# Page loads spread over the second block, raw weight halves loaded one stage ahead, 64-row products paired, and the samples' steps begun with the attention

## The reference

```
xn = rms_norm(x, norm_in)
u  = einsum('btd,dc->btc', xn, w_in)           # 2048 -> 12016 columns
u_a, u_b, u_m = split(u, [A_COLS, A_COLS + B_COLS])
o_a = rwkv7_mixer(u_a, ...)                    # 16 heads of 64, state S updated token by token
o_b = nsa_mixer(q, gates, cmp_kv, sel_kv, win_kv, ...)   # compressed, selected and window attention
h = x + (sig(gate_a) * (o_a @ w_pa) + sig(gate_b) * (o_b @ w_pb)) @ w_o
y = rms_norm(h, norm_out)
```

## Time and profile before

| | us |
|---|---|
| three runs | 2744.36, 2750.11, 2754.10 (median 2750.11) |
| the profiled execution | 2745.68 |
| its span | 2743.9 |

### The profile page before, as it was taken

The page is one execution under the profiler, slowest core; times in us unless marked ns, Lnnn a source line. Parts: engine busy times, 40 slices in busy tenths (PEclk is TensorE's granted clock), DMA queues, the critical chain, the costliest instruction groups (busy, mean ns, idle before and its releaser), DMA issues. The chain is left out here.

```text
span 2743.9 us, 50970 instructions
## 1 busy us (share of the span) xinstructions
PE 2391.9 (87%) x21174; PEld 2171.8 (79%) x21174; DVE 1192.3 (43%) x2330; ACT 797.1 (29%) x1495; POOL 439.7 (16%) x236
## 2 busy tenths in 40 slices
PE   5999999999999999778998789999815664999996
PEld 4998989898888989678997778888703334999996
DVE  4244544545454544336776434444414334443223
ACT  4342333333332332112221154445301112232211
POOL 0000000000000000000110049999800000000000
PEclk8999999999999999989999889999957885999998
DMA  3221212122121222166665422222175714332332
GB/s 121 91 84 61 71 62 76 64 76 76 56 81 61 71 73 79 59 203 210 209 224 183 147 58 79 60 76 67 56 237 176 222 47 162 140 140 106 103 110 89
DMA packets 123373, 299.56 MB, mean 109 GB/s; under 512 B 23962, under 2 KB 37028, under 8 KB 117412
## 3 DMA queue, kind: packets, MB, share of 16 engines
q1 hardware_dynamic: 104820, 252.93, 28.0%
q0 software_dynamic: 7360, 29.74, 3.1%
q10 hardware_dynamic: 10992, 14.05, 1.4%
HBM read 259.45 MB, written 45.54 MB: 111 GB/s over the span
## 5 line engine op out<-in xcount | busy, mean ns | idle before, releaser
L164 PE MATMUL acc<-xh,w_hi 128*128 128x272 f32 x1824 | 415.2, 309 | 21.9 <-DVE xl L419 11.1
L146 DVE TENSOR_TENSOR w_lo<-w_raw,w_hi 128x1024 fp32r<-128x1024 f32 x166 | 203.1, 1224 | 504.0 <-ACT w_hi L137 485.0
L164 PE MATMUL acc<-xh,w_lo 128*128 128x272 f32 x1824 | 378.8, 289 | 0.0
L164 PE MATMUL acc<-xl,w_hi 128*128 128x272 f32 x1824 | 378.5, 289 | 0.0
L164 PEld LDWEIGHTS acc<-xh,w_hi 128*128 128x128 f32 x1824 | 286.0, 190 | 58.2 <-issue 32.7
L137 ACT ACTIVATE w_hi<-w_raw 128x1024 fp32r<-128x1024 f32 x188 | 198.5, 1056 | 415.5 <-DMA w_raw<-in_w_all 197.4
L164 PEld LDWEIGHTS acc<-xl,w_hi 128*128 128x128 f32 x1824 | 288.8, 190 | 0.0
L164 PEld LDWEIGHTS acc<-xh,w_lo 128*128 128x128 f32 x1824 | 287.2, 190 | 0.0
L164 PE MATMUL b_acc<-xh,w_hi 128*128 128x272 f32 x800 | 174.3, 300 | 48.1 <-DVE w_lo L146 28.6
L164 PEld LDWEIGHTS b_acc<-xh,w_hi 128*128 128x128 f32 x800 | 131.2, 197 | 51.1 <-DVE w_lo L146 30.0
L164 PE MATMUL b_acc<-xl,w_hi 128*128 128x272 f32 x800 | 170.6, 296 | 0.0
(11 more groups left out here) (397 smaller groups left out, 4374.7 us busy)
## 6 DMA issues: line engine op xcount, KB each, us to landing
w_raw<-in_w_all SPq DMA_DIRECT2D x188, 512.0 KB, 3.6
b_rows<-in_cmp_rows SPq DMA_DIRECT2D x128, 256.0 KB, 3.2
d_kv<-in_sel_kv SPq DMA_DIRECT2D x128, 256.0 KB, 2.8
m_w<-in_w_mo SPq DMA_DIRECT2D x32, 1024.0 KB, 5.8
m_gates<-tmp_uT SPq DMA_DIRECT2D x16, 544.0 KB, 3.8
out_s_win<-in_win_in POOLq DMA_DIRECT2D x8, 1016.0 KB, 5.8
tmp_uT<-ub POOLq DMA_DIRECT2D x24, 272.0 KB, 2.3
tmp_uT<-ub ACTq DMA_DIRECT2D x23, 272.0 KB, 2.1
```

The costliest lines, as they stand in the source:

```text
L146: eng.tensor_tensor(self.T.Wl[h % N_SPLIT][:, :, :], self.T.raw[h % N_RAW][:, :, :], self.T.Wh[h % N_SPLIT][:, :, :].bitcast(F32), ALU.sub ...
L164: ins = self.nc.tensor.matmul(acc[:, c, 0:HALF], w[:, k % KH, :], x[:, k, c * HALF:(c + 1) * HALF], start=(k == 0 and m == 0), stop=(k == ...
```

## The change

The changed kernel alters four things.

- The raw halves of the next block are loaded at the end of the block before (`h_load`, two more than `h_ahead`), and SP waits for them there (`landed`).
- In `rwkv`, the products that use 64 rows only are issued in turns on rows 0 to 63 and 64 to 127: `G` (L897) and `W2` (L932). The last pair's pieces shrink from 48 to 36, and 12 pieces are left for behind `var`.
- In `rest`, the pages of a sample are loaded four at a time, one group of four per half, and each behind the raw half's load. The constants come behind the first four. The pooling begins at half 4, not 3.
- In `attend_prompt`, keys and queries lie on both row halves, so that `S0` uses rows 0 to 63 and `S1` rows 64 to 127, one right behind the other. The first row is loaded by ACT, the samples' data by POOL, the values have a semaphore of their own; the samples' preparation on ACT and DVE comes ahead of the first row, and 12 pieces come ahead of the first score instead of 7.

```diff
-        self.h_ahead = min(self.h1 + 2, 2 * N_CHUNK)
+        self.h_ahead, self.h_load = (min(self.h1 + n, 2 * N_CHUNK) for n in (2, 2 + N_RAW))
         self.ready = 0 if first == 0 else 2
+        self.loaded = 0 if first == 0 else 2 + N_RAW
...
+    def landed(self, sp):
+        for j in range(N_RAW):
+            sp.wait_ge(self.w_in[j], 16 * len([h for h in range(self.h0 + self.loaded, self.h_load) if h % N_RAW == j]))
...
-        before = [m for m in range(self.ready, n + 1) if (m + self.h0) % N_RAW == h % N_RAW]
-        act.wait_ge(self.w_in[h % N_RAW], 16 * len(before))
+        before = [m for m in range(self.loaded, n + 1) if (m + self.h0) % N_RAW == h % N_RAW]
+        if before:
+            act.wait_ge(self.w_in[h % N_RAW], 16 * len(before))
...
+        at, span = 0, pair if i < 7 else pair - LAST_PIECES
         for name, b0, nb, eng, gap in PAIR_JOBS:
             at += gap
...
-            place[i, name] = at
+            place[i, name] = FIRST_PIECES + pair * i + at * span // pair
...
+            W.landed(sp)
...
-                background(place[i, "var"])
+                background(place[i, "var"] + (LAST_PIECES if i == 7 else 0))
...
-                def g_quarter(q):
-                    job(i, f"G{q}")
-                    hp = H[q // 2]
+                def g_half(q):
+                    job(i, f"G{2 * q}")
+                    job(i, f"G{2 * q + 1}")
                     for n in range(4):
-                        nn = 4 * (q % 2) + n
-                        ins = mm(bank[:, bank_of[i, f"G{q}"], n * P:(n + 1) * P],
-                                 BK[hp, nn, :, :].rearrange("p a c -> p (a c)"),
-                                 KR[hp, nn, :, :].rearrange("p a c -> p (a c)"), start=True, stop=True)
-                    done(ins)
-                g_quarter(0)
-                g_quarter(1)
+                        for h, hp in enumerate(H):
+                            ins = mm(bank[:, bank_of[i, f"G{2 * q + h}"], n * P:(n + 1) * P],
+                                     BK[hp, 4 * q + n, :, :].rearrange("p a c -> p (a c)"),
+                                     KR[hp, 4 * q + n, :, :].rearrange("p a c -> p (a c)"), start=True, stop=True)
+                            if n == 3:
+                                done(ins)
+                g_half(0)
...
-                for h, name in enumerate(("W2a", "W2b")):
-                    job(i, name)
-                    for n in range(NCH):
+                job(i, "W2a")
+                job(i, "W2b")
+                for n in range(NCH):
+                    for h, name in enumerate(("W2a", "W2b")):
                         ins = mm(bank[0:CH, bank_of[i, name], n * CH:(n + 1) * CH], mats["Tt"][H[h], n, :],
                                  mats["X2"][H[h], n, :], start=True, stop=True)
-                    done(ins)
+                        if n == NCH - 1:
+                            done(ins)
...
-UNIT_AT, UNIT_END, PROMPT_AFTER = 3, 47, 1
+UNIT_AT, UNIT_END, PROMPT_AFTER = 4, 47, 1
...
+            def pages(b, q):
+                if b >= 2 and q == 0:
                     sp.wait_ge(x_used, b - 1)
-                for p in range(N_PAGES):
+                for p in range(4 * q, 4 * q + 4):
                     page = sp.value_load(table[0:1, b * N_PAGES + p:b * N_PAGES + p + 1], min_val=0, max_val=N_POOL - 1)
                     sp.dma_start(X[b % 2][:, p, :, :], A["cmp_rows"][bass.ds(page, 1)].rearrange("a c s x -> (a c) s x"))\
                         .then_inc(rows_in[b % 2], 16)
             for h in range(W.h0, W.h1):
-                if h + 4 < W.h_ahead:
+                if h + 4 < W.h_load:
                     W.load(sp, h + 4)
-                if h - W.h0 < 2:
-                    pages(h - W.h0)
-                for b in range(2, DEC_B):
-                    if ended[b - 2] == h - W.h0:
-                        pages(b)
+                for b in range(DEC_B):
+                    q = h - W.h0 - (4 * b if b < 2 else ended[b - 2] + 1)
+                    if 0 <= q < 4:
+                        pages(b, q)
+                if h == W.h0:
+                    for dst, src in ((pos_s, "pos_s"), (pos_w, "pos_c"), (wbd, "wbd"), (w_kv, "w_kv")):
+                        sp.dma_start(dst[:], A[src]).then_inc(consts, 16)
+            W.landed(sp)
...
-PROMPT_PIECES, START_PIECES = PIECES * (N_CHUNK - KEY_CHUNKS), 7
+PROMPT_PIECES, START_PIECES = PIECES * (N_CHUNK - KEY_CHUNKS), 12
...
+        def load_row(eng, w):
+            g, r = ROWS[w]
+            j = w % 2
+            row = COL_Q + w * HD
+            for k in range(2):
+                eng.dma_start(q[j][k * HD:(k + 1) * HD, :], A["uT"][row:row + HD, 0:SEQ]).then_inc(row_in[j], 16)
+            eng.dma_start(bias[j][:, :], A["bias_p"][g, :, r, :]).then_inc(row_in[j], 16)
+            eng.dma_start(cbias[j][:, :, :], A["cbias_p"][g, :, N_TILE * r:N_TILE * (r + 1), :]).then_inc(row_in[j], 16)
...
+            load_keys(0)
+            load_values(0)
+            load_row(sp, 1)
...
+            load_samples(pool)
             between()
             samples_steps(pool, between)
...
+            load_row(act, 0)
+            c = COL_GATE - 48 * P
+            act.dma_start(gates[:, :, :], A["u_tok"][:, :, c:c + N_GATE]).then_inc(gates_in, 16)
+            background(4)
+            samples_act(act)
+            background(8)
+            act.wait_ge(gates_in, 16)
+            f(gates[:, :, :], gates[:, :, :], ACT.Sigmoid).then_inc(gates_ready, 1)
+            act.wait_ge(gates_ready, 1)
...
+            samples_dve(dve)
             row_maxes(0)
             maxes(0)
...
+                banks = [job(f"S{k}", u) for k in range(2)]
+                for k, rows in enumerate((slice(0, HD), slice(HD, P))):
+                    done(mm(banks[k][:, 0:keys(t)], q[w % 2][rows, t * P:(t + 1) * P], kT[w // REP % 2][rows, 0:keys(t)],
                             start=True, stop=True))
...
+                if t == 0 and w % REP == 0:
+                    pe.wait_ge(values_in[w // REP % 2], 16 * N_VALUES_IN * (w // REP // 2 + 1))
```

More of the change, by code:

```diff
@@ L216, in job_tables @@
     jobs = [(-1, *j) for j in FIRST_JOBS]
-    place, at = {}, FIRST_PIECES
+    place, pair = {}, sum(j[4] for j in PAIR_JOBS)
     for i, name, *_, where in jobs:
@@ L338, in background @@
             def background(upto):
-                while loads[0] < W.h_ahead and HALF_PIECES * (loads[0] - 4) <= upto:
+                while loads[0] < W.h_load and HALF_PIECES * (loads[0] - 4) <= upto:
                     W.load(sp, loads[0])
@@ L1026, in _ @@
             sp.dma_start(table[:, :], A["page_table"]).then_inc(table_in, 16)
-            for h in (W.h0 + 2, W.h0 + 3):
-                W.load(sp, h)
-            for dst, src in ((pos_w, "pos_c"), (wbd, "wbd"), (pos_s, "pos_s"), (w_kv, "w_kv")):
-                sp.dma_start(dst[:], A[src]).then_inc(consts, 16)
             sp.wait_ge(table_in, 16)
-            def pages(b):
-                if b >= 2:
+            def pages(b, q):
+                if b >= 2 and q == 0:
                     sp.wait_ge(x_used, b - 1)
-                for p in range(N_PAGES):
+                for p in range(4 * q, 4 * q + 4):
                     page = sp.value_load(table[0:1, b * N_PAGES + p:b * N_PAGES + p + 1], min_val=0, max_val=N_POOL - 1)
@@ L1276, in load @@
         eng.dma_start(tab[:, :, :], A["stab"]).then_inc(loaded, 16)
-        eng.dma_start(S[:, :, :], A["state"]).then_inc(loaded, 16)
+        eng.dma_start(S[:, :, :], A["state"]).then_inc(state_in, 16)
     def store(eng):
@@ L1288, in act_before @@
         f = nc.scalar.activation
-        act.wait_ge(loaded, 48)
+        act.wait_ge(loaded, 32)
         f(w[:, :, :], sw, ACT.Exp, scale=DECAY_SCALE).then_inc(act_done, 1)
@@ L1336, in dve_before @@
         vv.memset(eps[:, :], GN_EPS)
-        dve.wait_ge(loaded, 48)
+        dve.wait_ge(loaded, 32)
         link(tt(kraw[:, :, :], k, over_t(0), ALU.mult))
@@ L1434, in attend_prompt @@
         W = Projection(nc, A, T, acc, "a", KEY_CHUNKS, N_CHUNK)
-        q, bias = [sb(f"a_q{j}", [HD, SEQ]) for j in range(2)], [sb(f"a_bias{j}", [P, SEQ]) for j in range(2)]
+        q, bias = [sb(f"a_q{j}", [P, SEQ]) for j in range(2)], [sb(f"a_bias{j}", [P, SEQ]) for j in range(2)]
         cbias = [sb(f"a_cbias{j}", [P, N_TILE, N_CMP_PAD]) for j in range(2)]
-        kT = [sb(f"a_kT{j}", [HD, 2, SEQ]) for j in range(2)]
+        kT = [sb(f"a_kT{j}", [P, SEQ]) for j in range(2)]
         vv = [sb(f"a_v{j}", [P, 2, N_TILE, HD]) for j in range(2)]
@@ L1447, in attend_prompt @@
         out = [sb(f"a_out{j}", [P, N_TILE, REP, HD]) for j in range(2)]
-        row_in, group_in = [sem(f"a_row_in{j}") for j in range(2)], [sem(f"a_group_in{j}") for j in range(2)]
+        row_in, keys_in, values_in = ([sem(f"a_{n}{j}") for j in range(2)] for n in ("row_in", "keys_in", "values_in"))
         gates_in, gates_ready, zeroed = sem("a_gates_in"), sem("a_gates_ready"), sem("a_zeroed")
@@ L1491, in load_group @@
```

(26 more changed lines are left out.)

44 lines of the change are left out of this document (20 added, 24 removed).

## The result

The changed kernel takes 2652.05 us (median of four runs, 2649.62 to 2653.21) against 2751.64 for the kernel before (four runs): ratio 0.9636, 95% interval 0.9616 to 0.9657. The forecast was 2647, with 2620 to 2690 as its range. The profiled execution took 2649.62 us, with a span of 2647.8 against 2743.9.

What follows compares the result with a forecast made beforehand. It took TensorE (PE), busy 87%, as the bound. Terms of -55 (`rest`), -17 (`rwkv` pairing), -1 (last pair) and -28 (attention) sum to -101: 2745.68 to 2644.7 us, plus half of 4.4, forecast 2647, range 2620 to 2690.

Steps and rivals of the forecast that it cites:

- Pages in `rest`: In `rest`: pages in fours between raw halves end PE's waits behind SP's queue; -55 us, of 42.7 idle and 21.0 low clock.
- The fit that was doubted: In `rest`: DVE's 239.5 to 255.6 us of work fits PE's 258.6 over 43 halves, by only 1 to 7%.
- Rivals C and D: In `rest`: DVE or late pages pace it, 2670 us, chance 0.17; or short waits keep the clock low, 2780 us, 0.04.
- Pairing in `rwkv`: In `rwkv`: `G` and `W2` in turns on both row halves overlap, taking 13.0 and 6.0 us less; counted as -17.
- the deduction for shorter cover: In `rwkv`: shorter products cover less of DVE's work behind them, so -17 us was taken of 19.
- Rival B: In `rwkv` and attention: products on two row halves with the same 128 columns do not overlap; 2677 us, chance 0.12.
- Last pair and gap: End of `rwkv`: fewer pieces cost +4.6 us, twelve held back cut the gap from 19.4 to about 14; net -1.
- Attention: In `attend_prompt`: POOL's chain ends the block and its first step comes earlier, about 26 us in; -28 us, bounds -33 and -13.
- With PE starting some 7 us in: Attention's start: PE starts 7 us in instead of 10.7, so POOL's third low part is done at about 25.
- One of about 14 us at row 4, inside the 13 us of slack: In the attention: SP loads rows behind raw halves, so PE waits about 14 us at row 4, within its slack against POOL.
- the condition for the -30: In the attention: paired scores gain nothing by themselves, but are needed for POOL's end to move from 419.4 to 389.4 us.
- The second reading of that end, 380: In the attention: 64 units of 5.16 us behind twelve pieces put PE's end at about 380 us.

Runs made afterwards that it cites:

- e1: The changed kernel, but SP issues the 16 pages of a sample in one go again, at the half where the kernel before did: 2714.95 us.
- e2: The changed kernel with `G` and `W2` issued one row half after the other again, at the same places: 2666.99 us.
- e3: The changed kernel with both score products of a unit on rows 0 to 63, the window keys in their own tile: 2668.65 us.
- e4: The changed kernel with LAST_PIECES 0: the last pair keeps its 48 pieces and none stands behind `var`: 2653.92 us.
- e5: The changed kernel, but POOL issues the loads of the samples' data only when row 0 has landed: 2644.60 us.
- e7: The changed kernel, but ACT instead of SP loads rows 2 to 15, behind the exponentials of the row two before: 2641.86 us.
- e9: The changed kernel, but PE does the pieces first and then waits for a row's inputs, and ACT loads rows 2 to 15: 2633.56 us.

## Why the prediction was right, and where not

The total came out nearer than its terms. Up to the end of `rest` the change gained 8 us more than forecast, in the attention 13 less, and that these stand against each other is luck: 96 us measured, 101 forecast.

*Pages in `rest` (-55 forecast, -59.4).* Right in mechanism and nearly in size. PE's waits are gone, and e1 brings them back with nothing but the grouping and place of the pages in SP's queue. The fit that was doubted held: DVE was busy 248.3 us and PE never waited for it. At 230 GB/s and a share of 0.71 (274 and 0.83 in the window shown) some pages were late for DVE, 5.6 us in four waits, and none of it reached PE. The 4 us of difference are low clock that I had left in the block. Rivals C and D fall.

*Pairing in `rwkv` (-17, measured 8 x 2.5 = -20).* The full -19 that the ratio gave was right to about 1 us, and the deduction for shorter cover was not needed. The rule that row groups work side by side is the Trainium skill's ("TensorE: Matmul & The Clock Gate", "Part 3: Packing small matmuls — row/col tiling"). The trace now shows it for this form: 1.16 us for eight products of `G` where the estimate by that rule with perfect overlap was 1.03, and 1.13 for a score pair where half of 1.98 is 0.99. Rival B falls, by the after trace and by e2 and e3.

*Last pair and gap (-1, measured +3.4 - 4.5 = -1.1).* Both terms were each about 1 us too large, and e4 shows that they are two. The norm was misread on the way: the 6.44 us in the earlier trace rows are DVE's idle time, and DVE began 2 us behind PE's last product. The 5.6 us that the store was to move are what it moved (7.9 to 2.3), but the gap shrank by 4.5 only.

*Attention (-28, measured -15.0, near the end of its bounds).* This is the term that was mis-sized. The reading that POOL's chain ends the block was right. Two steps of the working failed:
- "With PE starting some 7 us in": it started 14.2 us in. I had taken row 0's landing without its company. The small loads of row 0 are now in flight together with 3 MB of samples' data issued in the same 3 us, and the 64 KB of `cbias` took 12.1 us to land. e5 takes the company away, the same load lands in 4.7 us, and the kernel gains 7.5. The first step came at 34.9 instead of 26: 8.9 us. In e5 PE starts 6.9 us in, as the working had it, and the first step is at 27.3, so 7.6 of the 8.9 are PE's late start.
- "One of about 14 us at row 4, inside the 13 us of slack": the wait came, 15.95 us, and PE's slack held it, but the wait left PE by another way. ACT's copy waits for PE's products, POOL for ACT's copy, and POOL, which had no slack, waited 8.9 us for copies in its chain instead of 2.15. That is 6.7 us, and e7 removes all waits for copies from the chain. Together 15.6 us, against the 15 that were missing from -30. With both steps mended (e9) POOL ends 387.8 us into the block, where the prediction had 389.4.

The pairing of the scores was priced as "the condition for the -30", and this held: without it rival B had -13 instead of -28, 15 us less, and e3 shows 16.6. PE's own end was not where the prediction had it. The slack of 13 us between the chains was really 5, since PE too started late and waited for rows; it ended 400 us into the block, not at 376. The second reading of that end, 380, doesn't follow from its terms either: 7 us, twelve pieces of 1.5 and 64 units of 5.16 are 355, and what comes behind them is not named.

No run takes the earlier loads, the earlier preparation or the twelve pieces ahead of the first score out of the change, so how the 15 us that the attention gained divide among these is open.

## What to carry to other kernels

In a queue that issues in order, count what stands ahead of the transfer that the bound engine needs next: here 16 cheap issues of 1.1 us against a lead of 12 us cost 59 us, 43 of them idle time and 17 low clock. An engine's slack does not contain its waits: ask who waits for that engine's products, because a wait that the slack hides there can come out on a chain without any (here 6.7 us). And where a block starts, let the loads that the first instructions need go alone, or let the engine first do the work that needs none.

## What the runs showed of the hardware

Products with 64 rows and 128 columns took 2.05 us for eight on one row half, 1.71 when the half changed after four, and 1.16 when it changed with each: it is not all or nothing. SP issued a page in 1.12 us in the groups of 16 and in 0.91 in groups of four (3.63 us). Transfers at a share of 0.83 and 274 GB/s over 60 us did not delay PE at all, though DVE waited 5.6 us for pages in the block. A 64 KB load landed in 12.1 us with 3 MB issued on another queue within 3 us, and in 4.7 when those were held back until it had landed.
